# Two request groups through a hybrid decoder layer: the last eight row blocks are squared and scaled by halves, and GpSimd multiplies the halves that are final early by the norm's weights

## Chip, cores, metric

One NeuronCore of a Trainium2 chip runs the whole program. The metric is the device time in microseconds (us) of one execution; less is better. Engines are named as in the profile: PE (TensorE), DVE (VectorE), ACT (ScalarE), POOL (GpSimd), SP (SyncE, which here only issues DMAs).

## What is computed

One decoder layer over 2048 prompt rows and 8 sample rows, width 1024, float32: a gated delta net and a gated MLP over chunks read one input projection, their joined output goes through `w_o` and is added to `x`; then comes a squared-ReLU MLP of width 4096, also added, and a last RMSNorm. Only the end matters here:

```
def rmsnorm(x, g):
    y = x * rsqrt(mean(x * x, axis=-1) + 1e-6)
    return y * g
x = x + square(relu(rmsnorm(x, norm_ffn_g) @ w_up)) @ w_down
y = rmsnorm(x, norm_f_g)            # y_prompt (2048 x 1024), y_sample (8 x 1024)
```

Every row of `x` needs the sum of squares of its whole 1024 elements before any element of it can be scaled; the multiplication by `norm_f_g` needs no such sum.

## The kernel before, in words

The last stage (`ffn`, from L1820) keeps the result in `acc`, 16 row blocks of 128 rows by 1024 columns (shown as `f_acc`). The product with `w_down` is made in 16 chunks `m` of 7 ticks `k` each: a seven-product scheme for 2 by 2 blocks, each product in three passes (`three_pass`, L116) of matmuls of 512 columns, some 5.44 us a tick. PE signals twice per tick (`y_ready`); DVE answers each with one `add(m, k, jj)` (L2471 to L2482), which adds a pair of PSUM banks into half of the columns of two row blocks and counts `y_added`. `OUT_OF` says which part a tick goes to. In the last chunk, m = 15, the parts of row blocks 8 to 15 become final as follows: columns 0 to 511 of blocks 8 to 11 after k = 1, columns 512 to 1023 of blocks 12 to 15 after k = 4, columns 512 to 1023 of blocks 8 to 11 after k = 5, columns 0 to 511 of blocks 12 to 15 after k = 6, the last tick. Blocks 0 to 7 are final before chunk 15 begins.

The final norm is woven into chunk 15, by program order alone:

- ACT squares a block with its sum along the row (`square_row`, L2347, the instruction is L2350) into a scratch tile `row_junk` that shows as `f_dn_raw`; the sum is left by a second short instruction. Blocks 0 to 7 come two at a time at k = 0 to 3, between the high cuts of the next operand (`z_cut_hi`, L2322). Then follow the sample rows `s_acc` (shown as `x_s`), and after k = 5 blocks 8 to 15 whole, the last four in two steps as `add(15, 6, 0)` and `add(15, 6, 1)` end.
- POOL turns sums into reciprocal roots for blocks 0 to 3, 4 to 7 and the sample rows, 14 tiny instructions each (`rsqrt`, L87).
- DVE does the low cuts (`z_cut_lo`, L2461), the adds, and `finish(row)` (L2490, L2491), one `scalar_tensor_tensor` over 1024 columns: `acc` times the row's root times `fgain` (shown as `ffn_gains`). Blocks 0 to 7 are finished in k = 3, 4 and 5. For blocks 8 to 15 DVE makes the roots itself, in three groups (`root`, L2494, 11 tiny instructions): 8 to 11 between the two adds of k = 6, then 12 and 13, then 14 and 15.
- SP stores block after block (`store_y`, L2042 to L2044), 512 KB each, each waiting for `fin_made` of its block. The sample rows (L2105) stand between block 7 and block 8. The program waits for all stores.

Of the kernel before, what the change touches and what calls it, by code (L numbers as in the profile page):

```python
# [86 lines left out]
def rsqrt(eng, sem, base, r, m, tmp, fused=False):  # L87

    n = 0

    def did(ins):
        nonlocal n
        n += 1
        ins.then_inc(sem, 1)
        eng.wait_ge(sem, base + n)

    did(eng.tensor_scalar(r.bitcast(I32), m.bitcast(I32), -0.5, float(0x5F3759DF), ALU.mult, ALU.add))
    for _ in range(3):  # L100
        if fused:
            did(eng.scalar_tensor_tensor(out=tmp, in0=r, scalar=-0.5, in1=r, op0=ALU.mult, op1=ALU.mult))
            did(eng.tensor_tensor(tmp, tmp, m, ALU.mult))
            did(eng.scalar_tensor_tensor(out=r, in0=tmp, scalar=1.5, in1=r, op0=ALU.add, op1=ALU.mult))
        else:
            did(eng.tensor_tensor(tmp, r, r, ALU.mult))
            did(eng.tensor_tensor(tmp, tmp, m, ALU.mult))
            did(eng.tensor_scalar(tmp, tmp, -0.5, 1.5, ALU.mult, ALU.add))
            did(eng.tensor_tensor(r, r, tmp, ALU.mult))


def dve_rsqrt(dve, sem, base, r, m, tmp):
    rsqrt(dve, sem, base, r, m, tmp, fused=True)
# [44 lines left out]
class Stage:  # L158
# [5 lines left out]
    def sb(self, name, shape, dt=F32):  # L164
        return self.stack.enter_context(self.nc.sbuf_tensor(name, shape, dt))
# [1620 lines left out]
LEAD = 4  # L1786
T_SUMS_AT = {1: {11: (0, 1), 12: (2, 3), 13: (4, 5), 14: (6,), 15: (7,)}, 2: {PAIRS + 3 + x: (x,) for x in range(8)}}
CHUNKS = 16
GROUPS = 8
DSEQ = [(m, k) for m in range(CHUNKS) for k in range(K7)]  # L1790
OUT_OF = {0: (0, 0), 1: (0, 0), 2: (0, 1), 3: (1, 1), 4: (1, 1), 5: (0, 1), 6: (1, 0)}
# [28 lines left out]
def ffn(c, io, stack):  # L1820
# [6 lines left out]


    fss, fms, frt, frs = (sb("fin_" + x, [P, NCH + 1]) for x in ("ss", "ms", "rt", "rs"))
    row_ms, row_rt = sb("row_ms", [P, NBT]), sb("row_rt", [P, NBT])  # L1830
    ns_ss, ns_ms, ns_rt, ns_rs = (sb("ns_" + x, [P, 1]) for x in ("ss", "ms", "rt", "rs"))

# [11 lines left out]
    with ExitStack() as dn_stack:  # L1844
# [35 lines left out]
        f_squared fms_made f_refined fms_made_d f_refined_d fin_made y_stored""".split()  # L1880
# [60 lines left out]

    def z_loads_before(m, q):
        return sum(Z_SLOTS[x][y] == Z_SLOTS[m][q] for x in range(m) for y in range(4))

    def acc_rows(m, k, jj):
        t, d = OUT_OF[k]
# [3 lines left out]
    with nc.Block() as block:  # L1950

        @block.sync
        def _(eng):
# [87 lines left out]

            def store_y(row):  # L2042
                eng.wait_ge(s["fin_made"], row + 1)
                eng.dma_start(io["y_prompt"][0, row * P:(row + 1) * P, :], acc[:, row, :]).then_inc(s["y_stored"], 16)  # L2044

            eng.sem_inc(up_loaded[0], 32)
# [65 lines left out]
        def _(pool):  # L2112
# [128 lines left out]
            pool.wait_ge(s["f_squared"], 9)  # L2241
            pool.tensor_scalar(fms[0:n, cols], fss[0:n, cols], 1.0 / D, EPS, ALU.mult, ALU.add).then_inc(s["fms_made"], 1)
            pool.wait_ge(s["fms_made"], 3)
            rsqrt(pool, s["f_refined"], 2 * RSQRT_STEPS, frs[0:n, cols], fms[0:n, cols], frt[0:n, cols])

        @block.scalar
        def _(act):
# [99 lines left out]
            def square_row(row, col, src):  # L2347
                r = src.shape[0]
                wait(act, s["f_squared"], row if row < 8 else 8 if row == NCH else row + 1)
                act.activation(row_junk[0:r, :], src, ACT.Square, accum_out=fss[0:r, col:col + 1]).then_inc(s["f_squared"], 1)  # L2350
# [31 lines left out]
            for tick, (m, k) in enumerate(DSEQ):  # L2382
                if tick + 2 < len(DSEQ):
                    z_cut_hi(*DSEQ[tick + 2])
                if m == 0 and k + 2 < K7:
                    dn_cut_hi(0, k + 2)
                if (m, k) in DN_CUT_AT:
                    dn_cut_hi(*DN_CUT_AT[(m, k)])
                if (m, k) == (0, 4):
                    act.activation(zs[:].rearrange("p a f q -> p (a f q)").rearrange("p (b q) -> p b q", q=P), across(c.ident[:], 8),  # L2390
                                   ACT.Copy, scale=0.0).then_inc(s["zs_padded"], 1)
                    act.wait_ge(s["zs_padded"], 1)
                    zs_cut_hi(0)
                if m % 2 and k == 5 and m + 1 < CHUNKS:
                    zs_cut_hi(m // 2 + 1)
                if m == CHUNKS - 1 and k < 4:
                    for row in (2 * k, 2 * k + 1):
                        act.wait_ge(s["y_added"], 2 * (K7 * (CHUNKS - 2) + 6) + 2)
                        square_row(row, row, acc[:, row, :])
                    if k == 0:  # L2400
                        act.wait_ge(s["s_added"], 2 * GROUPS)
                        act.activation(s_low, s_acc[PAD:PAD + n, :], ACT.Copy).then_inc(s["low_moved"], 1)
            act.wait_ge(s["s_summed"], 1)
            square_row(NCH, NCH, s_acc[0:n, :])
            act.wait_ge(s["y_added"], 2 * (K7 * (CHUNKS - 1) + 5) + 2)
            for row in range(8, NCH):
                if row >= 12:
                    act.wait_ge(s["y_added"], 2 * (K7 * (CHUNKS - 1) + 6) + (row - 12) // 2 + 1)
                square_row(row, row, acc[:, row, :])

        @block.vector
        def _(dve):
# [54 lines left out]
            def zs_cut_lo(g):  # L2467
                dve.wait_ge(s["zs_hi"], g + 1)
                dve.tensor_tensor(zs[:, g % 2, :, PAD:PAD + n], zs_raw[:, g % 2], zs[:, g % 2, :, 0:n].bitcast(F32), ALU.subtract).then_inc(s["zs_lo"], 1)
# [24 lines left out]
            def root(i, row, after):  # L2494
                cols = slice(row, after)
                dve.wait_ge(s["f_squared"], after + 1)
                dve.tensor_scalar(fms[:, cols], fss[:, cols], 1.0 / D, EPS, ALU.mult, ALU.add).then_inc(s["fms_made_d"], 1)
                dve.wait_ge(s["fms_made_d"], i + 1)
                dve_rsqrt(dve, s["f_refined_d"], i * DVE_RSQRT_STEPS, frs[:, cols], fms[:, cols], frt[:, cols])
                dve.wait_ge(s["f_refined_d"], (i + 1) * DVE_RSQRT_STEPS)  # L2500

            w_cut_lo(0)
            for i in range(3):
# [33 lines left out]
            for tick, (m, k) in enumerate(DSEQ):  # L2537
                if m % 2 and k == 0:
                    add_sample(m // 2)
                if tick + 2 < len(DSEQ):  # L2540
                    z_cut_lo(*DSEQ[tick + 2])
                if m == 0 and k + 2 < K7:
                    dn_cut_lo(0, k + 2)
                if (m, k) in DN_CUT_AT:
                    dn_cut_lo(*DN_CUT_AT[(m, k)])
                if (m, k) == (0, 4):
                    zs_cut_lo(0)
                if m % 2 and k == 5 and m + 1 < CHUNKS:
                    zs_cut_lo(m // 2 + 1)
                add(m, k, 0)  # L2550
                if m == CHUNKS - 1 and k == 6:
                    root(0, 8, 12)
                add(m, k, 1)
                if m == CHUNKS - 1:
                    if k == 1:
                        dve.wait_ge(s["low_moved"], 1)
                        dve.tensor_tensor(s_acc[0:n, :], s_acc[0:n, :], s_low, ALU.add).then_inc(s["s_summed"], 1)
                    if k == 3:
                        dve.wait_ge(s["fgain_loaded"], 16)
                        dve.wait_ge(s["f_refined"], RSQRT_STEPS)  # L2560
                    if k == 5:
                        dve.wait_ge(s["f_refined"], 2 * RSQRT_STEPS)
                    for row in {3: (0, 1), 4: (2, 3), 5: (4, 5, 6, 7)}.get(k, ()):
                        finish(row)
            dve.wait_ge(s["f_refined"], 3 * RSQRT_STEPS)
            dve.scalar_tensor_tensor(out=s_acc[0:n, :], in0=s_acc[0:n, :], scalar=frs[0:n, NCH:NCH + 1], in1=fgain[0:n, :],
                                     op0=ALU.mult, op1=ALU.mult).then_inc(s["s_final"], 1)
            for row in range(8, 12):
                finish(row)
            for i, row in ((1, 12), (2, 14)):  # L2570
                root(i, row, row + 2)
                finish(row)
                finish(row + 1)

        @block.tensor
        def _(pe):
# [205 lines left out]
```

## Time and profile before

| | |
|---|---|
| median of 3 runs | 2376.34 us (2373.47 to 2377.32) |
| profiled execution, its own time | 2378.51 us |
| its span, first to last instruction | 2376.8 us |
| PE busy | 2297.5 us (97% of the span) |
| DVE busy | 1587.5 us (67%) |
| ACT busy | 1003.3 us (42%) |
| POOL busy | 779.8 us (33%) |
| granted TensorE clock, mean | 0.982 |

The span is what the rows are timed in: each row's start is counted from the first instruction. Between the profiled time and the span lie 1.7 us that no row shows. A row's duration is from the instruction's start on its engine to its end, so it contains time in which the instruction has been started and is held up; consecutive instructions of one engine overlap by some 0.1 us, so the cadence of a run of equal instructions is the distance between starts.

### The profile page before, as it was taken

How to read it: one execution, taken by the hardware profiler on the slowest of the kernel's cores; microseconds unless marked ns; L12 is line 12 of the kernel's file. 1: busy time of each engine (PE TensorE's matmuls, PEld its weight loads, DVE VectorE, ACT ScalarE, POOL GpSimd, SP SyncE). 2: the span in 40 equal slices, each digit the busy share in tenths (PEclk: the TensorE clock that was granted, in tenths of full speed). 3: DMA queues.
4: the chain of work that ended last, by engine and by line, in shares of the span. 5: the costliest groups of instructions: out<-in, count | busy, mean ns of one | idle time of the engine just before them, and what ended most of it. 6: DMA issues, size and time to landing. Idle time of an engine off the chain costs nothing.

```text
span 2376.8 us, 34154 instructions
## 1 busy us (share of the span) xinstructions
PE 2297.5 (97%) x12708; PEld 2100.6 (88%) x12708; DVE 1587.5 (67%) x2317; ACT 1003.3 (42%) x1959; POOL 779.8 (33%) x663
## 2 busy tenths in 40 slices
PE   7999999999899999969999999999999999999995
PEld 5999999999888888769999999999888888888884
DVE  6536564487676666586657644644678877897788
ACT  5333332211344344246667666766622322222233
POOL 4000001000122333254464543343534443434342
PEclk9999999999899999989999999999999999999998
DMA  5022334331655544337654543463452313231303
GB/s 181 27 81 89 103 101 143 118 106 45 221 177 157 152 134 133 120 116 243 191 173 136 179 134 122 133 212 125 158 183 80 98 43 98 82 90 44 98 27 142
DMA packets 304056, 296.72 MB, mean 125 GB/s; under 512 B 41212, under 2 KB 243296, under 8 KB 300556
## 3 DMA queue, kind: packets, MB, share of 16 engines
q1 hardware_dynamic: 303892, 294.54, 39.5%
q8 instruction: 102, 1.67, 0.3%
q14 instruction: 62, 0.51, 0.1%
HBM read 205.15 MB, written 89.44 MB: 124 GB/s over the span
## 4 chain that ended last, share of the span: by engine, by line
PE 50%; DVE 4%; ACT 1%; issue 1%; POOL 1%; DVEq 0%; ACTq 0%; POOLq 0%
PE bank L120 16%; PE bank L121 16%; PE bank L122 16%; DVE f_h_cut L2420 1%; PE bank L2580 1%; DVE f_up_cut L2416 1%; PE bank L2646 1%; PE bank L2648 1%; ACT f_h_cut L2276 1%; DVE f_acc L2491 1%; DVE f_part L2456 0%; DVE f_acc L2482 0%; ACT f_part L2303 0%; DVE xn L2450 0%; DVE xn L2516 0%
## 5 line engine op out<-in xcount | busy, mean ns | idle before, releaser
L120 PE MATMUL bank<-f_h_cut,f_up_cut 128*128 128x344 f32 x1344 | 438.1, 326 | 16.4 <-DVE f_up_cut L2416 6.7
L121 PE MATMUL bank<-f_h_cut,f_up_cut 128*128 128x344 f32 x1344 | 434.0, 323 | 0.0
L122 PE MATMUL bank<-f_h_cut,f_up_cut 128*128 128x344 f32 x1344 | 431.2, 321 | 0.0
L120 PE MATMUL bank<-f_dn_cut,f_z_cut 128*128 128x512 f32 x896 | 349.8, 390 | 3.6 <-ACT f_z L2307 2.8
L121 PE MATMUL bank<-f_dn_cut,f_z_cut 128*128 128x512 f32 x896 | 349.4, 390 | 0.0
L122 PE MATMUL bank<-f_dn_cut,f_z_cut 128*128 128x512 f32 x896 | 349.4, 390 | 0.0
L120 PE MATMUL bank<-h_hi,w_lo 128*128 128x412 f32 (+1 forms) x960 | 337.3, 351 | 0.0
L121 PE MATMUL bank<-h_lo,w_hi 128*128 128x412 f32 (+1 forms) x960 | 336.3, 350 | 0.0
L122 PE MATMUL bank<-h_hi,w_hi 128*128 128x412 f32 (+1 forms) x960 | 336.1, 350 | 0.0
L2482 DVE TENSOR_TENSOR f_acc<-bank,f_acc 128x1024 f32<-128x1024 f32 x224 | 269.1, 1217 | 93.9 <-PE bank L122 93.8
L120 PEld LDWEIGHTS bank<-f_h_cut,f_up_cut 128*128 128x128 f32 x1344 | 255.0, 190 | 20.4 <-DVE f_up_cut L2416 12.8
L122 PEld LDWEIGHTS bank<-f_h_cut,f_up_cut 128*128 128x128 f32 x1344 | 255.1, 190 | 0.0
L121 PEld LDWEIGHTS bank<-f_h_cut,f_up_cut 128*128 128x128 f32 x1344 | 254.6, 189 | 0.0
L2416 DVE TENSOR_TENSOR f_up_cut<-f_up_sum,f_up_cut 128x512 fp32r<-128x512 f32 x192 | 151.1, 788 | 98.5 <-ACT f_up_cut L2258 98.2
L120 PEld LDWEIGHTS bank<-f_dn_cut,f_z_cut 128*128 128x128 f32 x896 | 168.6, 188 | 42.0 <-issue 6.6
L122 PEld LDWEIGHTS bank<-f_dn_cut,f_z_cut 128*128 128x128 f32 x896 | 168.6, 188 | 35.2
L121 PEld LDWEIGHTS bank<-f_dn_cut,f_z_cut 128*128 128x128 f32 x896 | 168.6, 188 | 34.8
L121 PEld LDWEIGHTS bank<-h_lo,w_hi 128*128 128x128 f32 x960 | 181.3, 189 | 0.7
L120 PEld LDWEIGHTS bank<-h_hi,w_lo 128*128 128x128 f32 x960 | 181.4, 189 | 0.5
L122 PEld LDWEIGHTS bank<-h_hi,w_hi 128*128 128x128 f32 x960 | 181.1, 189 | 0.4
L2322 ACT ACTIVATE f_z_cut<-xn 128x1024 fp32r<-128x1024 f32 x68 | 72.3, 1064 | 248.9 <-PE bank L122 248.9
L420 POOL TENSOR_TENSOR xn<-xn,ga 128x512 f32<-128x512 f32 x16 | 16.7, 1043 | 353.6 <-DMA xn<-g_dram 353.6
(453 smaller groups left out, 4151.9 us busy)
## 6 DMA issues: line engine op xcount, KB each, us to landing
z_dram<-f_z SPq DMA_DIRECT2D x96, 344.0 KB, 2.2
p_dram<-ffn_gains SPq DMA_DIRECT2D x24, 1024.0 KB, 4.6
xn<-z_dram SPq DMA_DIRECT2D x44, 512.0 KB, 3.7
f_dn_raw<-in_w_down_dram SPq DMA_DIRECT2D x32, 512.0 KB, 6.4
up_raw<-in_w_up_dram SPq DMA_DIRECT2D x25, 512.0 KB, 4.1
up_raw<-in_w_in_dram SPq DMA_DIRECT2D x24, 512.0 KB, 5.7
up_raw<-p_dram SPq DMA_DIRECT2D x48, 256.0 KB, 5.2
f_up_raw<-in_w_up_dram SPq DMA_DIRECT2D x24, 512.0 KB, 4.5
```

Of the source, the lines that this page charges most:

```text
L120: pe.matmul(out, wl, xh, start=start and k == 0, stop=False, skip_group_check=skip)
L121: pe.matmul(out, wh, xl, start=False, stop=False, skip_group_check=skip)
L122: last = pe.matmul(out, wh, xh, start=False, stop=stop and k == n - 1, skip_group_check=skip)
L2276: act.activation(hc[:, k, 0], h_source(k), ACT.Copy).then_inc(s["h_hi"], 1)
L2322: act.activation(ring[tick % 3][:, 0], z_source(m, k), ACT.Copy).then_inc(s["z_hi"], 1)
L2416: dve.tensor_tensor(wc[:, at % K7, 1], w_source(u, k), wc[:, at % K7, 0].bitcast(F32), ALU.subtract).then_inc(s["w_lo"], 1)
L2420: dve.tensor_tensor(hc[:, k, 1], h_source(k), hc[:, k, 0].bitcast(F32), ALU.subtract).then_inc(s["h_lo"], 1)
L2482: dve.tensor_tensor(dst, heads(pair_of(m, k, jj), 2), dst, ALU.add).then_inc(s["y_added"], 1)
L2491: dve.scalar_tensor_tensor(out=acc[:, row, :], in0=acc[:, row, :], scalar=frs[:, row:row + 1], in1=fgain, op0=ALU.mult, op1=ALU.mult).then ...
L2580: last = pe.transpose(turn_bank(i, half)[:, q * r:(q + 1) * r], src[0:r, (4 * half + q) * P:(4 * half + q + 1) * P], c.ident[0:r, 0:r])
L2646: low = lambda: pe.matmul(bank[0:PAD, :], zs[:, g % 2, f, 0:PAD], dn[k][:, 1, q, :], start=False, stop=False, skip_group_check=True)
L2648: both = lambda: pe.matmul(bank[0:2 * PAD, :], zs[:, g % 2, f, :], dn[k][:, 0, q, :], start=i == 0, stop=i == len(pairs) - 1, skip_group_c ...
```

## The change

Blocks 8 to 15 are treated by halves of 512 columns. For each block the half that is final first is called early (`early_half`: columns 0 to 511 of blocks 8 to 11, columns 512 to 1023 of blocks 12 to 15), the other late.

- ACT: the sample rows are squared at k = 3 (before: after k = 6 of the loop). The early halves of 8 to 11 are squared at k = 4, those of 12 to 15 at k = 5. After the loop ACT squares the eight late halves, as their adds end, and then scales the eight early halves by the root (`finish_half`), in place.
- POOL: after the sample rows' root, two multiplications of four early halves each, 128 x 2048 elements, by the final weights, in place; each counts `gained`.
- DVE: `finish` of block 4 moves from k = 5 to k = 4; the sample rows are finished in k = 5. Before the last two adds stand two tiny instructions (`root_starts`) that turn the early sums into mean plus epsilon. `root(0)`, between the two adds of k = 6, is for blocks 8 to 11, `root(1)` for 12 to 15; each begins with one instruction that adds the late sums. Then `finish_late` over 512 columns in place of `finish` over 1024.
- SP: `store_y(row)` for rows 8 and on waits for `fin_halves` too. Order of stores and their size stay.

```
+            for d in range(2):
+                rows, cols = slice(8 + 4 * d, 12 + 4 * d), slice(d * 512, (d + 1) * 512)
+                pool.wait_ge(s["f_squared"], SQ_EARLY + 4 * d + 4)
+                pool.tensor_tensor(acc[:, rows, cols], acc[:, rows, cols], across(fgain[:, cols], 4), ALU.mult).then_inc(s["gained"], 1)
...
-            act.wait_ge(s["s_summed"], 1)
-            square_row(NCH, NCH, s_acc[0:n, :])
-            act.wait_ge(s["y_added"], 2 * (K7 * (CHUNKS - 1) + 5) + 2)
+                if m == CHUNKS - 1 and k == 3:
+                    act.wait_ge(s["s_summed"], 1)
+                    square_row(SQ_SAMPLE, s_acc[0:n, :], fss[0:n, NCH:NCH + 1])
+                if m == CHUNKS - 1 and k in (4, 5):
+                    squares_of_halves(k)
             for row in range(8, NCH):
-                if row >= 12:
-                    act.wait_ge(s["y_added"], 2 * (K7 * (CHUNKS - 1) + 6) + (row - 12) // 2 + 1)
-                square_row(row, row, acc[:, row, :])
+                late_square(row)
+            act.wait_ge(s["gained"], 2)
+            for d in range(2):
+                act.wait_ge(s["f_refined_d"], (d + 1) * DVE_RSQRT_STEPS)
+                for row in range(8 + 4 * d, 12 + 4 * d):
+                    finish_half(row)
...
+            def finish_half(row):
+                act.activation(early_half(row), early_half(row), ACT.Copy, scale=frs[:, row:row + 1]).then_inc(s["fin_halves"], 1)
...
+                if (m, k) == (CHUNKS - 1, 6):
+                    root_starts(0)
+                    root_starts(1)
                 add(m, k, 0)
-                if m == CHUNKS - 1 and k == 6:
-                    root(0, 8, 12)
+                if (m, k) == (CHUNKS - 1, 6):
+                    root(0)
                 add(m, k, 1)
...
-                    for row in {3: (0, 1), 4: (2, 3), 5: (4, 5, 6, 7)}.get(k, ()):
+                    for row in {3: (0, 1), 4: (2, 3, 4), 5: (5, 6, 7)}.get(k, ()):
                         finish(row)
...
             for row in range(8, 12):
-                finish(row)
-            for i, row in ((1, 12), (2, 14)):
-                root(i, row, row + 2)
-                finish(row)
-                finish(row + 1)
+                finish_late(row)
+            root(1)
+            for row in range(12, NCH):
+                finish_late(row)
...
             def store_y(row):
                 eng.wait_ge(s["fin_made"], row + 1)
+                wait(eng, s["fin_halves"], row - 7)
```

`late_square(row)` waits for `y_added` of k = 5 (blocks 8 to 11) or k = 6 (12 to 15) and squares 512 columns into `late_ss`; `finish_late(row)` is the `scalar_tensor_tensor` of `finish` over the late half; `across(ap, 4)` repeats the 512 weights for the four blocks.

## Rows read from the trace of the kernel before

**Rows 1.** Chain that ended last: start us, us, engine, tile, line.
```profile
2346.65 0.24 PE bank L122
...
2371.53 1.20 DVEq L1950
```

**Rows 2.** Timeline of DVE: start, us, engine, line, operation, out<-in, shape, count.
```profile
2345.36 1.21 DVE L2482 TENSOR_TENSOR f_acc<-bank,f_acc 128x1024 f32<-128x1024 f32 x1
2346.99 1.22 DVE L2482 TENSOR_TENSOR f_acc<-bank,f_acc 128x1024 f32<-128x1024 f32 x1 [0.42 <-PE bank L122]
2348.13 4.86 DVE L2491 SCALAR_TENSOR_TENSOR f_acc<-f_acc,f_fin_rs,ffn_gains 128x1024 f32<-128x1024 f32 x4
2352.91 1.21 DVE L2482 TENSOR_TENSOR f_acc<-bank,f_acc 128x1024 f32<-128x1024 f32 x1
2354.05 0.16 DVE L2497 TENSOR_SCALAR f_fin_ms<-f_fin_ss 128x4 f32<-128x4 f32 x1
...
2356.27 1.23 DVE L2482 TENSOR_TENSOR f_acc<-bank,f_acc 128x1024 f32<-128x1024 f32 x1
...
2358.60 4.85 DVE L2491 SCALAR_TENSOR_TENSOR f_acc<-f_acc,f_fin_rs,ffn_gains 128x1024 f32<-128x1024 f32 x4
```

**Rows 3.** Timeline of ACT, squares of blocks 8, 14 and 15.
```profile
2348.25 1.06 ACT L2350 ACTIVATE f_dn_raw<-f_acc 128x1024 f32<-128x1024 f32 x1 [10.11 <-DVE f_acc L2482]
...
2357.53 1.06 ACT L2350 ACTIVATE f_dn_raw<-f_acc 128x1024 f32<-128x1024 f32 x1 [0.98 <-DVE f_acc L2482]
...
2358.77 1.06 ACT L2350 ACTIVATE f_dn_raw<-f_acc 128x1024 f32<-128x1024 f32 x1
2359.73 0.19 ACT L2350 ACTIVATION_READ_ACCUMULATOR f_dn_raw<-f_acc 128x1 f32 x1
```

**Rows 4.** Timeline of SP: the store of block 8.
```profile
2359.89 0.36 SPq L2044 DMA_DIRECT2D out_y_prompt_dram<-f_acc  x1
```

**Rows 5.** Stretches: length, PE, PEld, DVE, ACT, POOL busy, clock, DMA share, GB/s.
```profile
2360.80:2366.10 5.30, 0.00 (x0) 0.00 (x0) 4.84 (x15) 0.00 (x0) 0.00 (x0) 0.50 0.96 390
...
2375.10:2375.50 0.40, 0.00 (x0) 0.00 (x0) 0.00 (x0) 0.00 (x0) 0.00 (x0) 0.50 0.00 0
```

**Rows 6.** Timeline of POOL: end of the sample rows' root.
```profile
2344.36 1.12 POOL L106 TENSOR_TENSOR f_fin_rt<-f_fin_rs 8x1 f32<-8x1 f32 x1
...
2346.09 0.18 POOL L109 TENSOR_TENSOR f_fin_rs<-f_fin_rs,f_fin_rt 8x1 f32<-8x1 f32 x1
```

**Rows 7.** Groups by line and shape (busy us, mean ns), POOL, 0 to 1400.
```profile
L1510 POOL TENSOR_TENSOR gg<-xn,o_gain 128x512 f32<-128x512 f32 x16 | 20.6, 1290 | 1.2 <-DMA v_gain<-in_v_norm_g_dram 1.2
...
L420 POOL TENSOR_TENSOR xn<-xn,ga 128x512 f32<-128x512 f32 x16 | 16.7, 1043 | 353.6 <-DMA xn<-g_dram 353.6
```

**Rows 8.** The same groups of POOL, from 1400 to the end.
```profile
L2172 POOL TENSOR_TENSOR xn<-xn,ffn_gains 128x1024 f32<-128x1024 f32 x4 | 9.6, 2406 | 10.7 <-DVE f_z_cut L2461 10.7
```

**Rows 9.** Timeline of DVE about 2207, in chunk 12 of the same stage.
```profile
2204.20 2.34 DVE L2482 TENSOR_TENSOR f_acc<-bank,f_acc 128x1024 f32<-128x1024 f32 x2
2206.46 1.21 DVE L2461 TENSOR_TENSOR f_z_cut<-xn,f_z_cut 128x1024 fp32r<-128x1024 f32 x1
2207.59 3.42 DVE L2465 TENSOR_TENSOR f_dn_cut<-f_dn_raw,f_dn_cut 128x1024 fp32r<-128x1024 f32 x1
```

**Rows 10.** Timeline of POOL in the same stretch.
```profile
2203.31 3.27 POOL L2161 TENSOR_TENSOR up_raw<-xn,f_z_spare 128x1024 f32<-128x1024 f32 x1 [5.83 <-DVE f_z_cut L2461]
2206.72 3.21 POOL L2164 TENSOR_TENSOR xn<-ffn_gains,xn 128x1024 f32<-128x1024 f32 x1
```

**Rows 11.** Timeline of DVE about 1079: a row scaling.
```profile
1079.12 1.88 DVE L2450 SCALAR_TENSOR_TENSOR xn<-xn,x_rs,ffn_gains 128x1024 f32<-128x1024 f32 x1
```

**Rows 12.** Timeline of POOL in the same stretch.
```profile
1078.36 1.56 POOL L2123 TENSOR_TENSOR f_up_sum<-f_up_sum,f_up_raw 128x512 f32<-128x512 f32 x1
```

**Rows 13.** Groups of DVE, 0 to 1400: a scaling of 512 columns.
```profile
L1406 DVE SCALAR_TENSOR_TENSOR vbn<-bank,mx_rs,v_gain 128x512 f32<-128x512 f32 x16 | 11.9, 743 | 0.0
```

**Rows 14.** Groups of ACT, 1400 to the end: 512 columns, 1024 columns.
```profile
L2258 ACT ACTIVATE f_up_cut<-f_up_raw 128x512 fp32r<-128x512 f32 x30 | 18.6, 621 | 0.0
...
L2350 ACT ACTIVATE f_dn_raw<-f_acc 128x1024 f32<-128x1024 f32 x16 | 16.9, 1057 | 13.1 <-DVE f_acc L2482 12.5
```

More of the change, by code:

```diff
@@ L1788 @@
 CHUNKS = 16
+SQ_SAMPLE, SQ_EARLY, SQ_LATE = 8, 9, 17
 GROUPS = 8
@@ L1829, in ffn @@
     fss, fms, frt, frs = (sb("fin_" + x, [P, NCH + 1]) for x in ("ss", "ms", "rt", "rs"))
+    late_ss = sb("fin_late_ss", [P, NBT])
     row_ms, row_rt = sb("row_ms", [P, NBT]), sb("row_rt", [P, NBT])
@@ L1879, in ffn @@
         low_moved s_summed s_final s_stored
-        f_squared fms_made f_refined fms_made_d f_refined_d fin_made y_stored""".split()
+        f_squared fms_made f_refined fms_made_d f_refined_d fin_made fin_halves gained y_stored""".split()
     s = {nm: sem("f_" + nm) for nm in names}
@@ L1943, in z_loads_before, with early_half, late_half @@
         return sum(Z_SLOTS[x][y] == Z_SLOTS[m][q] for x in range(m) for y in range(4))
+    def early_half(row):
+        d = (row - 8) // 4
+        return acc[:, row, d * 512:(d + 1) * 512]
+    def late_half(row):
+        d = 1 - (row - 8) // 4
+        return acc[:, row, d * 512:(d + 1) * 512], fgain[:, d * 512:(d + 1) * 512]
     def acc_rows(m, k, jj):
@@ L2240, in _ @@
             cols = slice(NCH, NCH + 1)
-            pool.wait_ge(s["f_squared"], 9)
+            pool.wait_ge(s["f_squared"], SQ_SAMPLE + 1)
             pool.tensor_scalar(fms[0:n, cols], fss[0:n, cols], 1.0 / D, EPS, ALU.mult, ALU.add).then_inc(s["fms_made"], 1)
@@ L2345, in zs_cut_hi, with square_row, squares_of_halves, late_square @@
                 act.activation(zs[:, g % 2, :, 0:n], zs_raw[:, g % 2], ACT.Copy).then_inc(s["zs_hi"], 1)
-            def square_row(row, col, src):
+            def square_row(at, src, out):
                 r = src.shape[0]
-                wait(act, s["f_squared"], row if row < 8 else 8 if row == NCH else row + 1)
-                act.activation(row_junk[0:r, :], src, ACT.Square, accum_out=fss[0:r, col:col + 1]).then_inc(s["f_squared"], 1)
+                wait(act, s["f_squared"], at)
+                act.activation(row_junk[0:r, 0:src.shape[1]], src, ACT.Square, accum_out=out).then_inc(s["f_squared"], 1)
+            def squares_of_halves(k):
+                d = 0 if k == 4 else 1
+                for row in range(8 + 4 * d, 12 + 4 * d):
+                    act.wait_ge(s["y_added"], 2 * (K7 * (CHUNKS - 1) + (4 if d else 1)) + 2)
+                    square_row(SQ_EARLY + row - 8, early_half(row), fss[:, row:row + 1])
+            def late_square(row):
+                act.wait_ge(s["y_added"], 2 * (K7 * (CHUNKS - 1) + (5 if row < 12 else 6)) + (row % 4) // 2 + 1)
+                square_row(SQ_LATE + row - 8, late_half(row)[0], late_ss[:, row - 8:row - 7])
+            def finish_half(row):
+                act.activation(early_half(row), early_half(row), ACT.Copy, scale=frs[:, row:row + 1]).then_inc(s["fin_halves"], 1)
             w_cut_hi(0)
@@ L2398, in _ @@
                         act.wait_ge(s["y_added"], 2 * (K7 * (CHUNKS - 2) + 6) + 2)
-                        square_row(row, row, acc[:, row, :])
+                        square_row(row, acc[:, row, :], fss[:, row:row + 1])
                     if k == 0:
@@ L2402, in _ @@
                         act.activation(s_low, s_acc[PAD:PAD + n, :], ACT.Copy).then_inc(s["low_moved"], 1)
-            act.wait_ge(s["s_summed"], 1)
-            square_row(NCH, NCH, s_acc[0:n, :])
-            act.wait_ge(s["y_added"], 2 * (K7 * (CHUNKS - 1) + 5) + 2)
-            for row in range(8, NCH):
-                if row >= 12:
-                    act.wait_ge(s["y_added"], 2 * (K7 * (CHUNKS - 1) + 6) + (row - 12) // 2 + 1)
-                square_row(row, row, acc[:, row, :])
+                if m == CHUNKS - 1 and k == 3:
[3 more added lines that the diff above has]
+                    squares_of_halves(k)
+            for row in range(8, NCH):
+                late_square(row)
+            act.wait_ge(s["gained"], 2)
+            for d in range(2):
+                act.wait_ge(s["f_refined_d"], (d + 1) * DVE_RSQRT_STEPS)
+                for row in range(8 + 4 * d, 12 + 4 * d):
+                    finish_half(row)
         @block.vector
@@ L2492, in finish, with root_starts, root, finish_late @@
                                          op0=ALU.mult, op1=ALU.mult).then_inc(s["fin_made"], 1)
-            def root(i, row, after):
-                cols = slice(row, after)
-                dve.wait_ge(s["f_squared"], after + 1)
+            def root_starts(d):
+                cols = slice(8 + 4 * d, 12 + 4 * d)
+                dve.wait_ge(s["f_squared"], SQ_EARLY + 4 * d + 4)
                 dve.tensor_scalar(fms[:, cols], fss[:, cols], 1.0 / D, EPS, ALU.mult, ALU.add).then_inc(s["fms_made_d"], 1)
-                dve.wait_ge(s["fms_made_d"], i + 1)
-                dve_rsqrt(dve, s["f_refined_d"], i * DVE_RSQRT_STEPS, frs[:, cols], fms[:, cols], frt[:, cols])
-                dve.wait_ge(s["f_refined_d"], (i + 1) * DVE_RSQRT_STEPS)
+            def root(d):
+                cols = slice(8 + 4 * d, 12 + 4 * d)
+                dve.wait_ge(s["f_squared"], SQ_LATE + 4 * d + 4)
+                dve.wait_ge(s["fms_made_d"], 2 + d)
+                dve.scalar_tensor_tensor(out=fms[:, cols], in0=late_ss[:, 4 * d:4 * d + 4], scalar=1.0 / D, in1=fms[:, cols],
+                                         op0=ALU.mult, op1=ALU.add).then_inc(s["fms_made_d"], 1)
+                dve.wait_ge(s["fms_made_d"], 3 + d)
+                dve_rsqrt(dve, s["f_refined_d"], d * DVE_RSQRT_STEPS, frs[:, cols], fms[:, cols], frt[:, cols])
+                dve.wait_ge(s["f_refined_d"], (d + 1) * DVE_RSQRT_STEPS)
+            def finish_late(row):
+                half, gains = late_half(row)
+                dve.scalar_tensor_tensor(out=half, in0=half, scalar=frs[:, row:row + 1], in1=gains,
+                                         op0=ALU.mult, op1=ALU.mult).then_inc(s["fin_made"], 1)
             w_cut_lo(0)
@@ L2560, in _ @@
                         dve.wait_ge(s["f_refined"], RSQRT_STEPS)
+                    if k == 4:
+                        dve.wait_ge(s["f_refined"], 2 * RSQRT_STEPS)
+                    for row in {3: (0, 1), 4: (2, 3, 4), 5: (5, 6, 7)}.get(k, ()):
+                        finish(row)
                     if k == 5:
-                        dve.wait_ge(s["f_refined"], 2 * RSQRT_STEPS)
-                    for row in {3: (0, 1), 4: (2, 3), 5: (4, 5, 6, 7)}.get(k, ()):
-                        finish(row)
-            dve.wait_ge(s["f_refined"], 3 * RSQRT_STEPS)
-            dve.scalar_tensor_tensor(out=s_acc[0:n, :], in0=s_acc[0:n, :], scalar=frs[0:n, NCH:NCH + 1], in1=fgain[0:n, :],
-                                     op0=ALU.mult, op1=ALU.mult).then_inc(s["s_final"], 1)
-            for row in range(8, 12):
-                finish(row)
-            for i, row in ((1, 12), (2, 14)):
-                root(i, row, row + 2)
-                finish(row)
-                finish(row + 1)
+                        dve.wait_ge(s["f_refined"], 3 * RSQRT_STEPS)
+                        dve.scalar_tensor_tensor(out=s_acc[0:n, :], in0=s_acc[0:n, :], scalar=frs[0:n, NCH:NCH + 1], in1=fgain[0:n, :],
+                                                 op0=ALU.mult, op1=ALU.mult).then_inc(s["s_final"], 1)
+            for row in range(8, 12):
+                finish_late(row)
+            root(1)
+            for row in range(12, NCH):
+                finish_late(row)
         @block.tensor
```

## Prediction

> **What bounds the kernel now.** I read the chain of waits first, to see who holds the end. PE's last link is at 2346.65 and the last link is a DVE wait at 2371.53 [rows 1]: for the last 30 us the program is DVE, and then a store. TensorE's work doesn't matter for this change; after 2353 PE is idle. Second, the timeline of DVE [rows 2]: it has no gap after 2348.13; scalings of 1.20 us (4.78 us from the start of four to the next start), adds of 1.14 (2352.91 to 2354.05), and a root of 2.22 (2354.05 to 2356.27). Third, ACT [rows 3]: it stood idle for 10.11 us ahead of block 8's square, and then follows DVE. Fourth, the stores [rows 4, 5]: block 8 is issued at 2359.89, and four blocks' data are out at 2366.1, at 390 GB/s over 5.3 us with the DMA engines busy 0.96 of it. So four blocks take 6.2 us, of which about 1.0 is the way to the first byte, and each more costs 1.3. The last data are out by 2375.1, and the span ends at 2376.8: 1.7 us. Fifth, POOL, which the change gives new work: its last root runs into DVE's scalings [rows 6].
>
> **What goes, comes and moves.** I follow the clock from 2345.36, where the two kernels part [rows 2].
>
> DVE, as if nothing held it. `finish(4)` comes ahead of `add(15,5,0)`: that add starts at 2345.36 + 1.20 = 2346.56, the next at 2347.70 (its banks were ready at 2346.99 [rows 2], so the old wait of 0.42 us is filled), and `finish(5)` is asked for at 2348.84. Three scalings (3.59), the sample rows (1.19: in [rows 2] the add from 2356.27 takes 1.14 and the scalings begin at 2358.60), two tiny root starts (0.39, two of eleven parts of 2.22): `add(15,6,0)` starts at 2354.0. Then 1.14, the root 2.22, and `add(15,6,1)` of 1.23 ends at 2358.6. Before, it ended at 2357.5; the tail behind it is where the gain is: eight scalings of 1.20 become eight of about 0.66 (a scaling of 512 columns has 0.74 us [rows 13], one of 1024 has 1.27, since four with three overlaps of 0.08 make 4.86 [rows 2]; I take off the same 0.53), and one root of three is gone. By DVE alone the end would come 6.6 us sooner.
>
> ACT. The early squares (four of about 0.80 us, twice) lie in the idle 10.11 us [rows 3]: nothing. A half square costs 0.80: 1.24 from start to start [rows 3] less the 0.44 between ACT's 1024 and 512 columns [rows 14]; the last, with its sum, 1.15 - 0.44 = 0.71. After `add(15,6,1)` two late squares stand ahead of the first `finish_half` in ACT's order: 2358.6 + 0.80 + 0.71 = 2360.1; block 8's early half is then scaled in 0.62 [rows 14], and its store goes out at 2360.8. If ACT's cover were gone, each half square would cost its 0.80.
>
> Stores. Here most of DVE's gain goes: no block from 8 on can be stored before the last squares are done, and behind 2360.8 all eight follow, since ACT readies one per 0.6 us and DVE's second root (2363.4) and late halves are done by 2366, while the DMA engines want 1.3 us a block. The end is 2360.8 + 6.2 + 4 x 1.3 + 1.7 = 2373.9: **2.9 us sooner**, if POOL's new work holds nobody. The old kernel had the same eight stores spread over the last 17 us. SP's other waits and the sample store, now ahead, cost nothing: SP is not late at any of them.
>
> POOL. The root of the sample rows ended at 2346.27 [rows 6]. `finish(4)` now holds one of its tiny instructions as `finish(3)` held L106 (1.12 us instead of 0.18 [rows 6]), so the first multiplication starts at about 2347.3. Its price: no row has 128x2048. 512 columns with a repeated operand, a product, take 1.29 us [rows 7], 1024 take 2.41 [rows 8]: 1.12 per 512, so 4.64 for 2048. Below, four times the cheapest 512 (1.04, one operand constant along each head [rows 7]) are 4.17; above, four times 1.29 are 5.16. I take 4.64, since both operands are full tiles as in [rows 8]. This is 9.3 us of POOL; if it ran beside DVE it would be done at 2356.6, before ACT asks at 2360.1, and cost nothing.
>
> The Trainium skill prices a two-input GpSimd instruction in another way: the page "GPSIMD Engine Reference", section "2.1 Instruction dispatch", gives about 2.5 cycles per element as the floor, since both operands come through one read port, and 1.2 GHz as clock; an estimate from that is 4.27 us for 2048, by which the end would come 0.7 us sooner than with my price. Rows 8 and 7 are above it, as a floor allows.
>
> It does not run beside DVE. [Rows 9, 10]: DVE's L2465 has 3.42 us instead of 1.21. It started at 2207.59, POOL's L2164 ended at 2209.93, and L2465 ended at 2211.01, 1.08 later. That is a stop until POOL is through, not sharing. The reverse stands beside it: L2164 was started at 2206.72 while L2461 (2206.46) ran, and has 3.21 instead of 2.41, its 2.34 counted from DVE's next start. And that pair shows who goes next: both wanted to run when L2461 was done, and POOL did. DVE adds out of PSUM are free of this: the two at 2204.20 have their usual 2.34 beside L2161 [rows 9, 10]. For a scaling, the instruction in question: L2450 started at 1079.12 and ended at 1081.00, 1.08 after POOL's L2123 (1079.92) [rows 11, 12]. The skill states the same rule (page "SBUF — State Buffer", section "SBUF: two separate sides"): GpSimd and a DVE instruction with two SBUF inputs take one port pair as an exclusive lock for the whole instruction. By that rule, the trace agrees.
>
> So: multiplication 1 runs from 2347.3 to 2351.9. `finish(5)`, asked for at 2348.84, waits; DVE's next start comes 1.00 after POOL's end, 2352.9 (before it would have been 2350.0). Multiplication 2 is waiting by then (its squares are done by 2346.3) and gets in as L2164 did: it ends 4.64 - 0.07 after DVE's start, at 2357.5, and `finish(6)` waits through it. `finish(7)` starts at 2358.5 instead of 2351.2: **7.3 us later**. Queued behind on DVE are `finish(7)`, the sample rows, and both adds of the last tick, whose banks have been full since about 2352.5; behind those ACT's late squares and every store from block 8. Nothing fills it. The sum: 2373.9 + 7.3 = 2381.2, that is 4.4 us over the span of 2376.8.
>
> The sum is against the profiled execution (2378.51, span 2376.8); the median of the runs is 2376.34. I carry the difference over: 2376.34 + 4.4 = **2380.7 us**, 0.19% slower.
>
> **The rivals.**
> (a) Slower, past what can be told: the same blocking with a dearer multiplication. Its operands are four pieces of 512 columns with a jump between; if each piece is paid as an instruction of its own, it is 5.16 us, two such add 1.0: 2381.8. It decides from 4.8 us each on (4.75 us, 0.2%, is the bound). For it: every POOL row of 512 has a fixed part of about 0.17 us (1.29 - 1.12). Against: those of 1024 are two pieces too, and follow the line.
> (b) Not slower: POOL holds nobody, because it gets the port only in gaps, or its work falls beside the adds. Then 2376.34 - 2.9 = 2373.4. Against: the rows above, on both kinds of DVE instruction. For: an earlier start, by 1.5 us or so, would put part of multiplication 1 under the adds; it can't, the root is ahead of it in POOL's order.
> (c) Half of it: after multiplication 1 DVE keeps the port through its scalings, and POOL gets in at `add(15,6,0)`, about 2356.6, until 2361.2; the root behind that add, tiny instructions with two SBUF inputs, waits. It would start at 2361.2 instead of 2355.2: 6.1 instead of 7.3 us, 2379.5. Against: [rows 9, 10].
> (d) The change does not do what it says if the early squares are not early. ACT has 10.11 us free and needs 6.4, so they are.
>
> **How the numbers follow.** About 0.2%, 4.75 us, is what a measurement of this kernel can tell from no change. Forecast, 0.62: 2380.7, with its price from 4.17 to 4.8 us 2379.8 to 2381.0, and the runs of one kernel lie up to 2.9 us from their median. Rival (a) 0.18, (c) 0.06, (b) 0.10, the rest, unknown waits on either side, 0.04. The range 2377.5 to 2383.0 leaves out (b), the unknown and the ends of the scatter, no more than 0.2 together. The forecast lies 0.35 us under the bound, so I split it: 0.22 slower by over 0.2%, 0.40 within. With (a) 0.16 and 0.02 from the rest, slower is 0.40. Faster by over 0.2% asks for more than (b) can give, since the stores stand in a row: 0.04. Within: 0.56.
>
> **What would show it.** In the profile after: two POOL multiplications, the second with about 5.5 us by its row (0.9 of waiting); `finish(5)` with 4.2 us or so and `finish(6)` with 5.6 instead of 1.27; the first store of a block from 8 on at about 2368.1; DMA engines busy without a gap for 10.4 us from 2369 on; and an end 1.7 us after that. If the scalings have 1.27 us throughout, the blocking is wrong and (b) holds. If POOL's first product has over 4.8 us, (a). If the stores have gaps between them, the store step is wrong, and DVE's second root sets the end.

## The result

The changed kernel takes 2381.52 us (median of 9 runs, 2379.93 to 2382.62) against 2377.22 us for the kernel before (9 runs, 2373.47 to 2379.17): a ratio of 1.002, 95% interval 1.0011 to 1.0029, so slower by 0.11 to 0.29%. The forecast was 2380.7 us, 4.4 us slower; the medians lie 4.3 us apart. The forecast time itself is 0.8 us too low, and all of that is the base: it was counted from 2376.34 us, and the kernel before has 2377.22 over nine runs. That 4.3 comes so close to 4.4 is partly luck, since the interval of the ratio reaches from 2.6 to 6.9 us.

Executions of one kernel differ by a few us, and much of this lies ahead of the end: the last matmul starts at 2351.93 in the profiled execution of the kernel before, and anywhere from 2347.66 to 2355.97 in those of the other kernels below, whose PE program is the same. It takes 0.39 us in each. What follows is therefore also compared as **the tail**, from the one profiled execution of each kernel: the span less the end of the last matmul. No kernel below holds up PE near its end: in the last 37 us before the last matmul, two matmuls never start more than 0.24 us apart in any of the ten traces, so nothing is hidden in front of the tail. Before it is 2376.80 - 2352.32 = 24.5 us, after it is 28.5 us, 4.0 more. The last matmul after, timeline of PE:

```profile
2351.64 0.39 PE L122 MATMUL bank<-f_dn_cut,f_z_cut 128*128 128x512 f32 x1
```

### The profile page after: what moved, and what is told of

It reads as the page before. It is cut to its first block, busy times and chain, and to the rows that moved or that the text cites. A ratio compares the mean times of both kernels' runs of the same rounds, so it can differ in the third digit from the quotient of the medians.

```text
span 2380.5 us, 34192 instructions
## 1 busy us (share of the span) xinstructions
PE 2298.7 (97%) x12708; PEld 2101.2 (88%) x12708; DVE 1588.2 (67%) x2308; ACT 1011.3 (42%) x1983; POOL 790.5 (33%) x665
## 4 chain that ended last, share of the span: by engine, by line
PE 50%; DVE 4%; issue 1%; ACT 1%; POOL 1%; DVEq 0%; ACTq 0%; POOLq 0%
PE bank L120 16%; PE bank L121 16%; PE bank L122 16%; DVE f_h_cut L2453 1%; PE bank L2628 1%; DVE f_up_cut L2449 1%; PE bank L2694 1%; DVE f_acc L2524 1%; PE bank L2696 1%; ACT f_h_cut L2291 1%; DVE f_part L2489 0%; DVE f_acc L2515 0%; ACT f_part L2318 0%; DVE xn L2483 0%; DVE f_acc L2544 0%
## 5 line engine op out<-in xcount | busy, mean ns | idle before, releaser
L420 POOL TENSOR_TENSOR xn<-xn,ga 128x512 f32<-128x512 f32 x16 | 16.7, 1044 | 351.8 <-DMA xn<-g_dram 351.8
```

## The profile after

The page's busy times show nothing of it: DVE has the same 1588 us, POOL 11 more. A row's time includes the time in which it is held, so what the half-size scalings save on DVE is filled up again by what it stands still.

```profile
span 2380.5 us, 34192 instructions
...
PE 2298.7 (97%) x12708; PEld 2101.2 (88%) x12708; DVE 1588.2 (67%) x2308; ACT 1011.3 (42%) x1983; POOL 790.5 (33%) x665
```

The timeline of DVE from the last add of k = 5 on (start, us, engine, line, operation, shapes, count), where [rows 2] of before had four scalings in 4.86 us:

```profile
2347.40 1.21 DVE L2515 TENSOR_TENSOR f_acc<-bank,f_acc 128x1024 f32<-128x1024 f32 x1
2348.53 4.18 DVE L2524 SCALAR_TENSOR_TENSOR f_acc<-f_acc,f_fin_rs,ffn_gains 128x1024 f32<-128x1024 f32 x1
...
2352.64 5.51 DVE L2524 SCALAR_TENSOR_TENSOR f_acc<-f_acc,f_fin_rs,ffn_gains 128x1024 f32<-128x1024 f32 x1
...
2359.26 1.27 DVE L2615 SCALAR_TENSOR_TENSOR x_s<-x_s,f_fin_rs,ffn_gains 8x1024 f32<-8x1024 f32 x1
2360.46 0.22 DVE L2530 TENSOR_SCALAR f_fin_ms<-f_fin_ss 128x4 f32<-128x4 f32 x2
2360.60 1.21 DVE L2515 TENSOR_TENSOR f_acc<-bank,f_acc 128x1024 f32<-128x1024 f32 x1
...
2363.94 1.23 DVE L2515 TENSOR_TENSOR f_acc<-bank,f_acc 128x1024 f32<-128x1024 f32 x1
2365.08 2.73 DVE L2544 SCALAR_TENSOR_TENSOR f_acc<-f_acc,f_fin_rs,ffn_gains 128x512 f32<-128x512 f32 x4
...
2369.97 2.74 DVE L2544 SCALAR_TENSOR_TENSOR f_acc<-f_acc,f_fin_rs,ffn_gains 128x512 f32<-128x512 f32 x4
```

The same stretch on POOL, its two products:

```profile
2347.00 4.63 POOL L2259 TENSOR_TENSOR f_acc<-f_acc,ffn_gains 128x2048 f32<-128x2048 f32 x1
...
2351.58 5.49 POOL L2259 TENSOR_TENSOR f_acc<-f_acc,ffn_gains 128x2048 f32<-128x2048 f32 x1
```

Read them side by side. `finish(5)` is started at 2348.53, the first product ends at 2351.63, and `finish(5)` ends 1.08 later, at 2352.71. The second product is started at 2351.58, held by `finish(5)` for 0.86 us (5.49 against the first one's 4.63), and ends at 2357.07; `finish(6)`, started at 2352.64, ends 1.08 after it, at 2358.15. An instruction that needs 1.27 us by itself has 4.18 and 5.51: 2.9 and 4.2 us of standing still, 7.1 together. The add at 2347.40 runs beside the first product in its usual 1.21.

Behind that, the stores. First the stretch view (length, busy time and count of PE, PEld, DVE, ACT, POOL, clock, DMA share, GB/s), then the store of block 8 and two of the last ones on SP:

```profile
2368.40:2378.80 10.40, 0.00 (x0) 0.00 (x0) 3.95 (x12) 3.34 (x6) 0.00 (x0) 0.50 1.00 397
2378.80:2380.40 1.60, 0.00 (x0) 0.00 (x0) 0.00 (x0) 0.00 (x0) 0.00 (x0) 0.50 0.00 0
```

```profile
2367.42 0.35 SPq L2055 DMA_DIRECT2D out_y_prompt_dram<-f_acc  x1
...
2372.91 2.41 SPq L2055 DMA_DIRECT2D out_y_prompt_dram<-f_acc  x2
```

Block 8 is stored at 2367.42, the DMA engines are then busy without a gap for 10.4 us, which is eight blocks, and the span ends 1.7 us after. DVE is through at 2372.71, as early as before (2372.73), and yet the program ends 3.7 us later: the end has passed from DVE to the stores. The chain of waits can't show this. It ends with a wait of 0.66 us and two scalings on DVE:

```profile
2370.72 0.66 DVEq L1960
2371.38 1.32 DVE f_acc L2544 x2
```

and is silent on the 7.8 us from there to the end of the span. Before, it stopped 4.1 us short of the end, which is about the time of one store with its 1.7 us behind it; 7.8 is more than one store takes. So a chain that stops well short of the end is a reason to look at the stores.

## Experiments

Two questions: does the loss come from the port that POOL's products hold, and is it the row of stores that takes most of what the halves gain? Tails are worked out as above. Four of the kernels leave something out, and are there only to be measured: without products and ACT's order leave out the final weights on the early halves of blocks 8 to 15, one product leaves them out on those of 12 to 15, and half stores leaves out the same weights and does not write half of the last eight blocks.

| kernel | last matmul starts | span | tail | forecast of the tail | median us | ratio to before, 95% |
|---|---|---|---|---|---|---|
| before | 2351.93 | 2376.8 | 24.5 | | 2377.22 | |
| changed | 2351.64 | 2380.5 | 28.5 | 28.9 | 2381.52 | 1.0011 to 1.0029 |
| without products | 2355.97 | 2377.7 | 21.3 | 21.6 | 2373.60 | 0.9981 to 1.0000 |
| one product | 2348.62 | 2373.2 | 24.2 | 24.5 | 2375.75 | 0.9991 to 1.0010 |
| eight pieces | 2350.01 | 2377.6 | 27.2 | 27.8 | 2379.74 | 1.0007 to 1.0026 |
| old kernel with products | 2347.66 | 2379.5 | 31.4 | 31.6 | 2382.17 | 1.0021 to 1.0047 |
| half stores | 2348.64 | 2366.0 | 17.0 | 16.9 | 2368.13 | 0.9948 to 0.9975 |
| ACT's order | 2351.20 | 2371.3 | 19.8 | 19.8 | 2372.33 | 0.9969 to 0.9987 |
| whole blocks | 2354.51 | 2377.2 | 22.3 | 22.3 | 2374.57 | 0.9979 to 0.9998 |
| whole blocks, earlier | 2347.94 | 2368.8 | 20.4 | 20.4 | 2373.28 | 0.9974 to 0.9991 |

How the forecast of the tail was made: for the changed kernel and the four under it, it is 24.5 plus the forecast difference in time to the kernel before; for the last four, it stands in the expectation as a time from the last matmul, or is 24.5 less the forecast gain. Each ratio is against the kernel before as it was timed beside that kernel: its median was 2377.22 beside the changed kernel, 2376.21 beside the next four and 2376.93 beside the last four. Set against these medians, the forecasts of the time were 4.4 us slower for the changed kernel (measured 4.3) and 7.1 slower for the old kernel with products (measured 6.0, from five runs).

### Without products

```
-            for d in range(2):
-                rows, cols = slice(8 + 4 * d, 12 + 4 * d), slice(d * 512, (d + 1) * 512)
-                pool.wait_ge(s["f_squared"], SQ_EARLY + 4 * d + 4)
-                pool.tensor_tensor(acc[:, rows, cols], acc[:, rows, cols], across(fgain[:, cols], 4), ALU.mult).then_inc(s["gained"], 1)
...
-            act.wait_ge(s["gained"], 2)
```

> The changed kernel without POOL's two products and without ACT's wait for them; it leaves out the final weights on the early halves of blocks 8 to 15. Everything else, the eight scalings on ACT among it, stays. Port theory (POOL's product stops DVE's two-input instructions): finish(5) and finish(6) are back at 1.27 us, the first store of block 8 comes 7.2 us sooner, and the median is about 2374.3, 2.9 under the kernel before and 7.2 under the changed one. Store theory beside it: still the eight stores stand in a row behind block 8 for 10.4 us, so the gain over the kernel before is 2.9 us, not the 6.6 us by which DVE alone ends sooner. Rival (the loss is ACT's, its squares and scalings in the way of the stores): the median stays within 1 us of the changed kernel's 2381.5.

The tail is 21.3 us, 7.1 under the changed kernel's. One line of the view by line (shortest, median, longest duration in ns) says that no scaling is held any more:

```profile
L2519 DVE SCALAR_TENSOR_TENSOR f_acc<-f_acc,f_fin_rs,ffn_gains x8: 1270/1273/1280, 2341.2 to 2355.3; 128x1024 f32<-128x1024 f32 x8
```

and the stores still fill 10.4 us:

```profile
2365.60:2376.00 10.40, 0.00 (x0) 0.00 (x0) 3.94 (x12) 3.33 (x6) 0.00 (x0) 0.50 1.00 397
```

So ACT's squares and scalings are not what was lost; without POOL's part the change is worth 3.2 us of tail. DVE's last scaling ended 2369.90 - 2356.36 = 13.5 us after the last matmul against 20.4 before, 6.9 sooner; less than half of that reaches the end.

### One product

```
-            for d in range(2):
+            for d in range(1):
...
-            act.wait_ge(s["gained"], 2)
+            act.wait_ge(s["gained"], 1)
```

> The changed kernel with the first product alone (early halves of 8 to 11); it leaves out the weights on the early halves of 12 to 15. Port theory: only finish(5) is held, for 2.9 us (product 4.63 us, of which 1.5 to 1.9 lie under the adds), so the median is 2374.3 + 2.9 = 2377.2, equal to the kernel before. The second product is dearer than the first since none of it lies under an add: 4.4 us. Rival (cost goes by POOL's busy time, half of it with half of the work): 2374.3 + 3.6 = 2377.9. Rival (one product at the start of the run is enough to lose it all): 2381.5.

```profile
L2524 DVE SCALAR_TENSOR_TENSOR f_acc<-f_acc,f_fin_rs,ffn_gains x8: 1272/1274/4179, 2333.9 to 2350.8; 128x1024 f32<-128x1024 f32 x8
```

One scaling of eight is held, for the 4179 ns that the changed kernel showed, and the tail is 24.2: 2.9 us for the first product, and so 4.2 for the second (28.5 - 24.2). The rival that goes by POOL's busy time would have 24.9; the medians alone could not tell the two apart, the tails do, and the row shows where the difference lies: 1.5 us of the first product run beside the two adds ahead of `finish(5)`.

### Eight pieces

```
-                pool.tensor_tensor(acc[:, rows, cols], acc[:, rows, cols], across(fgain[:, cols], 4), ALU.mult).then_inc(s["gained"], 1)
+                for row in range(8 + 4 * d, 12 + 4 * d):
+                    pool.tensor_tensor(acc[:, row, cols], acc[:, row, cols], fgain[:, cols], ALU.mult).then_inc(s["gained"], 1)
...
-            act.wait_ge(s["gained"], 2)
+            act.wait_ge(s["gained"], 8)
```

> The changed kernel with its two products cut into eight of 128x512, one a block; whole computation. Port theory with the turn going to the one that waits: DVE and POOL alternate, each of finish(5), finish(6), finish(7) and the sample rows is held for 1.2 us or so (rows of 2.4 instead of 1.27), two or three pieces fall beside the adds of the last tick, and one or two hold the tiny instructions of the root. Worked out from the start of POOL: 6.3 us late instead of 7.3, median 2380.5. Rival (what counts is POOL's total, now 8 x 1.29 = 10.3 instead of 9.3): 2382.5. Rival (DVE keeps the port once it has it): only the first piece holds DVE, the rest falls beside the adds: 2376 to 2378.

Timeline of DVE: two of the scalings, the sample rows, and the first instructions of the last tick.

```profile
2348.93 2.30 DVE L2525 SCALAR_TENSOR_TENSOR f_acc<-f_acc,f_fin_rs,ffn_gains 128x1024 f32<-128x1024 f32 x1
...
2351.15 2.28 DVE L2525 SCALAR_TENSOR_TENSOR f_acc<-f_acc,f_fin_rs,ffn_gains 128x1024 f32<-128x1024 f32 x1
...
2353.36 2.27 DVE L2616 SCALAR_TENSOR_TENSOR x_s<-x_s,f_fin_rs,ffn_gains 8x1024 f32<-8x1024 f32 x1
2355.55 1.29 DVE L2531 TENSOR_SCALAR f_fin_ms<-f_fin_ss 128x4 f32<-128x4 f32 x2
2356.76 1.21 DVE L2516 TENSOR_TENSOR f_acc<-bank,f_acc 128x1024 f32<-128x1024 f32 x1
...
2358.07 1.15 DVE L99 TENSOR_SCALAR f_fin_rs<-f_fin_ms 128x4 int32<-128x4 int32 x1
```

The pieces on POOL (shortest, median, longest duration in ns):

```profile
L2260 POOL TENSOR_TENSOR f_acc<-f_acc,ffn_gains x8: 1255/1766/2260, 2345.4 to 2357.9; 128x512 f32<-128x512 f32 x8
```

The two engines take turns, one piece and one scaling, as expected: each scaling has 2.3 us, of which 1.03 is waiting for a piece, and a piece that waits for a scaling has up to 2.26 instead of 1.26. The tail is 27.2 us, 1.2 under the changed kernel's, where the rival of POOL's total asked for 1.0 more and the one in which DVE keeps the port asked for several less. So on these rows the engine that waits gets the port next, in both directions. What POOL's work costs DVE is not its total: three of the eight pieces fall in whole or in part beside adds. What I had not expected is L2531 and L99: instructions with a single SBUF input, four elements long, and yet held as a scaling is (1.29 for two, where the changed kernel's pair has 0.22; 1.15 instead of 0.17).

### The old kernel with products

```
...
+            free = dn_raw[:, 2:4].rearrange("p a q t -> p (a q) t")
+            for d in range(2):
+                pool.tensor_tensor(free, free, across(fgain[:, 0:512], 4), ALU.mult).then_inc(s["gained"], 1)
...
```

> The kernel before, whole, with the two products added on POOL behind the sample rows' root, on tiles that nobody uses any more: nothing waits for them and they change no output. Port theory: they run from 2346.4 on, hold finish(4) or finish(5) and the one after it, and DVE is 7.1 us late behind them; that shows in full at the end, since there DVE sets it: 2377.2 + 7.1 = 2384.3. Rival (products cost only through what waits for them): 2377.2.

```profile
2343.86 3.92 DVE L2497 SCALAR_TENSOR_TENSOR f_acc<-f_acc,f_fin_rs,ffn_gains 128x1024 f32<-128x1024 f32 x1
...
2347.70 5.52 DVE L2497 SCALAR_TENSOR_TENSOR f_acc<-f_acc,f_fin_rs,ffn_gains 128x1024 f32<-128x1024 f32 x1
```

Nobody waits for these products and nobody reads them, and the tail is 31.4 us, 6.9 more than without them. The two held scalings have 2.65 and 4.25 us above their 1.27: 6.9, all of it at the end. This is the cost by itself, in a kernel where nothing else was changed. The medians have 6.0 us, with an interval (5.0 to 11.2) that holds 6.9 as well.

### Half stores

On top of the edit without products:

```
-                eng.dma_start(io["y_prompt"][0, row * P:(row + 1) * P, :], acc[:, row, :]).then_inc(s["y_stored"], 16)
+                w = D if row < 8 else 512
+                eng.dma_start(io["y_prompt"][0, row * P:(row + 1) * P, 0:w], acc[:, row, 0:w]).then_inc(s["y_stored"], 16)
```

> The changed kernel without the products (as in the run without them), and the stores of blocks 8 to 15 carry only their first 512 columns; the rest of those rows is not written. Store theory (behind block 8 the eight stores in a row set the end): with half of the bytes the end goes to the last late half on DVE plus one store, 4.4 us sooner than without products; from the last matmul's end 16.9 us instead of 21.3, median about 2369.2. Rival (the end waits for DVE's last instruction, as the chain of waits has it, and a fixed way behind it): no more than 0.7 us sooner, 2373.

The tail falls from 21.3 to 17.0. No engine does less, and half of the last stores' bytes are worth 4.3 us: what the chain of waits left out was the bound. DVE's last scaling ends 2362.57 - 2349.03 = 13.5 us after the last matmul, as it did without products, and the span now ends 3.5 us behind it instead of 7.8.

### ACT's order

On top of the edit without products:

```
-            for row in range(8, NCH):
-                late_square(row)
+            for row in range(8, 14):
+                late_square(row)
+            act.wait_ge(s["f_refined_d"], DVE_RSQRT_STEPS)
+            for row in range(8, 12):
+                finish_half(row)
+            late_square(14)
+            late_square(15)
...
```

> The changed kernel without the products, and ACT scales the early halves of 8 to 11 ahead of the late squares of 14 and 15 instead of behind them. Store theory: block 8 is stored 1.56 us sooner (then DVE's late half gates it), the row of eight stores moves with it, and the end too: 19.8 us from the last matmul instead of 21.3, median about 2372.1. Its price is a second root that waits 0.2 us, which nobody sees. Rival (the end waits for DVE's second root and the late halves of 12 to 15): no gain or 0.2 us of loss, 2373.6 to 2373.8.

The tail is 19.8, 1.6 us under that without products. ACT does the same instructions in another order, and DVE's last scaling is no sooner (2365.31 - 2351.59 = 13.7 us behind the last matmul, 13.5 without the new order). What moved is the start of the row of stores: block 8 is stored 6.7 us after the last matmul (2358.27) instead of 8.3 (2364.61 in the kernel without products). With that the row of stores is shown by both of the things that set its end, its length and its start.

### Whole blocks, and whole blocks earlier

The first keeps the early squares and the two roots, and takes both helpers away from the scaling. It also puts `root(0)` ahead of the last two adds. The second moves the scalings of blocks 0 to 7 into earlier ticks, and their stores on SP with them.

```
-            for row in range(8, 12):
-                finish_late(row)
+            for row in range(8, 12):
+                finish(row)
...
-                    for row in {3: (0, 1), 4: (2, 3, 4), 5: (5, 6, 7)}.get(k, ()):
+                    for row in {2: (0, 1), 3: (2, 3), 4: (4, 5), 5: (6, 7)}.get(k, ()):
```

> Whole computation: early and late squares and two roots as in the changed kernel, root(0) ahead of the last two adds, but nothing on POOL and no scaling on ACT; DVE finishes all eight blocks whole with one instruction of 1.20 us each, the sample rows after the adds. DVE has 21.5 us of work behind add(15,5,1) and no wait. If DVE sets the end again: last block issued about 18.0 us after the last matmul, end 22.3 us after it instead of 24.5 in the kernel before; median 2.2 under it, about 2374. Rival (the early squares bring nothing, all of the gain is in the halves): 2376.2.

> As the one with whole blocks, and blocks 0 and 1 are finished at k = 2, 2 and 3 at k = 3, 4 and 5 at k = 4, 6 and 7 at k = 5: DVE stood idle for 0.36 and 1.50 us ahead of the adds of k = 3, and these scalings fill it. The last scaling of a block under 8 is done 1.9 us sooner; end 20.4 us after the last matmul, median 4.1 under the kernel before, about 2372. Rival (adds that come later hold PSUM banks, and PE waits): PE's own end moves later by as much as DVE gains, 2374 or more.

Tails of 22.3 and 20.4 us, both as forecast. The eight stores of each, on SP, first of the one, then of the other, take 10.95 us from the first issue to the end of the last. DVE readies a block every 1.20 us with a root between, so the stores are spread out, no long row of them stands ahead of the store of block 15, and the end is DVE's again:

```profile
2362.31 10.95 SPq L2054 DMA_DIRECT2D out_y_prompt_dram<-f_acc  x8
```

```profile
2353.86 10.95 SPq L2054 DMA_DIRECT2D out_y_prompt_dram<-f_acc  x8
```

In the second kernel DVE doesn't wait for PE from k = 3 on; after the two scalings that came forward, the adds of k = 3 stand back to back:

```profile
2327.75 2.47 DVE L2514 SCALAR_TENSOR_TENSOR f_acc<-f_acc,f_fin_rs,ffn_gains 128x1024 f32<-128x1024 f32 x2
2330.14 1.22 DVE L2484 TENSOR_TENSOR f_z_cut<-ffn_gains,f_z_cut 128x1024 fp32r<-128x1024 f32 x1
2331.28 2.35 DVE L2505 TENSOR_TENSOR f_acc<-bank,f_acc 128x1024 f32<-128x1024 f32 x2
```

The rival, that PE waits for its banks, could not show in the tail, which begins at PE's end; but PE's matmuls run on without a gap up to there, at most 0.24 us from start to start, as in every other kernel.

It beats both kernels: 0.9983 of the kernel before (0.9974 to 0.9991), 3.7 us by the medians and 4.0 by the tails. All computation is in it. About half of the gain is that of the first of the two kernels, which has the early squares, one root fewer and the filled wait of 0.42 us ahead of the last add of k = 5 (these three were not tried apart); the rest comes from the earlier scalings.

## Why the prediction was right, point by point

- **Who sets the end of the old kernel.** DVE: products that touch nothing of its data, but hold it for 6.9 us, move the end by 6.9.
- **DVE without anything in its way.** A scaling of 512 columns has a cadence of 0.66 (four in 2.73), as taken. The last scaling was forecast 6.6 us sooner; without products it is 6.9 sooner. The early squares cost nothing that shows.
- **The stores take most of it.** Forecast 2.9 us left of the 6.6, measured 3.2; the two experiments on the stores' size and start moved the end by 4.3 and 1.6, forecast 4.4 and 1.5. Forecast from block 8's issue to the end: 6.2 + 5.2 + 1.7 = 13.1; after: 2380.48 - 2367.42 = 13.1.
- **Price of a product.** 4.64 worked out on the line through 512 and 1024 columns, 4.63 measured, which is the third point that the line did not have; rival (a), by pieces of 512, is out. The estimate of 4.27 from the Trainium skill's page "GPSIMD Engine Reference" (section "2.1 Instruction dispatch") is 0.36 too low as a price; as a floor it is not broken by the product. But the prediction's reading that all of [rows 7, 8] lie above that floor is wrong for one of them: L420 has 1.043 us for 512 columns, where the same figure gives an estimate of 1.067. Nothing in the sum rests on it.
- **Who holds whom.** `finish(5)` forecast 4.2, measured 4.18; `finish(6)` 5.6 and 5.51; second product 5.5 and 5.49; the turn goes to the one that waits, so rival (c) is out. Rival (b) is out by the rows and by the old kernel with products. The rule on the exclusive port pair, in the Trainium skill's page "SBUF — State Buffer" (section "SBUF: two separate sides"), agrees with the rows shown here: scalings with two SBUF inputs are held to the end of POOL's instruction, and adds out of PSUM are not held. The prediction gave it for two SBUF inputs only; the section also names VectorE instructions in a two-port performance mode, and no trace here shows in which mode the one-input L2531 and L99 ran.
- **The sum.** 7.3 forecast for both products, 7.1 by the tails; 7.3 - 2.9 = 4.4 forecast in all, 4.0 by the tails and 4.3 by the medians. The two misses do not offset each other: both make the loss smaller by the tails. The larger is the gain without products, 0.3 us too small, and nearly all of it is the term of the two root starts: charged with 0.39 us as two links of the root's chain, they take 0.14 (2360.46 to 2360.60 in the changed kernel); neither needs the other's result.
- **The chances.** Whether the loss is above or below 0.2% (4.75 us) was open, and still is: the interval of the ratio, 1.0011 to 1.0029, holds both.

## What to carry to other kernels

Before work is given to GpSimd, look at what VectorE does in that stretch. Here the part that ran beside adds out of PSUM was free, and the rest cost VectorE nearly all of its time: 4.2 us for a second product of 4.6. Cut into eight pieces it cost 1.2 us less, in the one case that was tried. Before work is spread over more engines at the end of a program, count what must be stored behind the first moment at which a store can begin: here eight blocks at 1.3 us each, which faster engines could not shorten. And give the critical engine's idle gaps, some ticks before the end, the work that is ready by then: that brought 1.9 us here, for no added instruction.

## What was not expected

A one-input instruction of DVE, SBUF to SBUF and four elements long, was held by POOL as well: 1.15 us for L99 in the kernel with eight pieces, 0.17 by itself. I had counted only those with two inputs.

SP's own time for a store grows when stores pile up: 0.36 us for block 8 in the kernel before [rows 4], and up to 1.17 in the changed one, by the line of its view (shortest, median, longest in ns):

```profile
L2055 SPq DMA_DIRECT2D out_y_prompt_dram<-f_acc x16: 332/349/1166, 2338.2 to 2374.2; - x16
```

It costs nothing here, since the DMA engines stay busy throughout (share 1.00 over the 10.4 us). What it would do to another transfer on that queue was not tried.
